# A decoder layer with expert retrieval: the top-16 searches spread over more slots, eight score tiles ahead of the first row group, and 16 KB of the residual stream lent to two more row buffers

## The reference, cut to what matters

```python
h2 = rmsnorm(x2) * (1 + sc2) + sh2
q  = h2 @ w_q                                  # 8 heads x two halves of 128
s1, s2 = scores of each half against 128 keys
v1, i1 = top_k(s1, 16); v2, i2 = top_k(s2, 16)
best, pos = top_k(all 256 sums v1 + v2, 16)    # 16 experts of 16384 for a token and head
gates = softmax(best)
act = gelu(einsum(u_tab[experts], h2))         # one row of 2048 of table u per expert
y   = sum(gates * act * v_tab[experts])        # one row of 2048 of table v per expert
out = rmsnorm(x2 + g2 * y)
```

## Time and profile before

| | |
|---|---|
| median of three runs | 1752.9 us |
| profiled execution | 1751.18 us, span 1749.4 us |
| mean granted clock of TensorE | 0.909 |
| busy: TensorE, VectorE, ScalarE, GpSimd | 1478.3, 1206.5, 542.8, 690.7 us |
| moved by DMA | 624.46 MB, mean 357 GB/s |
| queue of the gathers and of GpSimd's other loads (q0) | 427.52 MB |
| queue of SyncE's loads (q1) | 195.67 MB |

### The profile page before, as it was taken

The page is one execution under the profiler, slowest core; times in us unless marked ns, Lnnn a source line. Parts: engine busy times, 40 slices in busy tenths (PEclk is TensorE's granted clock), DMA queues, the critical chain, the costliest instruction groups (busy, mean ns, idle before and its releaser), DMA issues.

```text
span 1749.4 us, 20157 instructions
## 1 busy us (share of the span) xinstructions
PE 1478.3 (85%) x7320; PEld 980.5 (56%) x7320; DVE 1206.5 (69%) x2134; ACT 542.8 (31%) x1589; POOL 690.7 (39%) x626
## 2 busy tenths in 40 slices
PE   2979999989999998898999757656689899988874
PEld 2558987878788875666676434324333343333331
DVE  5877886879889988898454467768654555445463
ACT  3003442764311247343210146537421010101132
POOL 1000011000122354556676466555654454445461
PEclk9889999999999999999999876667789999998987
DMA  9999997849969679999999899998989999999996
GB/s 337 386 385 407 402 354 308 303 167 370 380 233 359 225 293 379 377 368 397 390 402 396 325 388 379 378 350 319 394 338 406 366 402 400 362 417 389 416 381 249
DMA packets 149806, 624.46 MB, mean 357 GB/s; under 512 B 33994, under 2 KB 38272, under 8 KB 86528
## 3 DMA queue, kind: packets, MB, share of 16 engines
q0 software_dynamic: 82976, 427.52, 62.6%
q1 hardware_dynamic: 66732, 195.67, 29.1%
HBM read 797.54 MB, written 2.10 MB: 457 GB/s over the span
## 4 chain that ended last, share of the span: by engine, by line
PE 31%; DMA 30%; DVE 24%; issue 6%; POOL 5%; ACT 3%; DVEq 1%; SPq 1%; POOLq 0%; ACTq 0%
DMA u_rows<-in_peer_u,expert 23%; DVE u_rows L2033 12%; PE ps L1167 6%; PE ps L1069 5%; PE ps L457 4%; PE ps L912 4%; DVE first_acc L486 3%; DMA v_rows<-in_peer_v,expert_rows 3%; POOL v_rows L801 3%; PE ps L906 2%; PE ps L1219 2%; PE ps L1134 2%; DMA ada_first<-in_w_ada 2%; PE ps L1204 2%; DMA u_rows<-in_peer_v,expert_rows 1%
## 5 line engine op out<-in xcount | busy, mean ns | idle before, releaser
L2033 DVE SCALAR_TENSOR_TENSOR u_rows<-u_rows,h 128x1024 f32<-128x1024 f32 (+1 forms) x416 | 595.3, 1469 | 377.9 <-DMA u_rows<-in_peer_u,expert 374.3
L801 POOL DMA_INDIRECT u_rows<-in_peer_u,expert x256 | 320.6, 1253 | 364.5 <-DVE u_rows L2033 289.5
L801 POOL DMA_INDIRECT v_rows<-in_peer_v,expert_rows x199 | 264.1, 1327 | 162.3 <-PE ps L1167 108.5
L1167 PE MATMUL ps<-v_rows,diag 128*32 128x512 f32 x1592 | 259.4, 693 | 65.1 <-DMA v_rows<-in_peer_v,expert_rows 35.6
L1219 PE MATMUL ps<-dense_rows,dense_weight 128*128 128x512 f32 x640 | 290.6, 612 | 14.9 <-DVE dense_sums L2112 8.2
L457 PE MATMUL ps<-h2T,dense_rows 128*128 128x256 f32 x1280 | 284.0, 383 | 4.2 <-ACT dense_weight L1565 4.1
L457 PEld LDWEIGHTS ps<-h2T,dense_rows 128*128 128x128 f32 x1280 | 243.4, 191 | 52.6 <-issue 17.9
L1219 PEld LDWEIGHTS ps<-dense_rows,dense_weight 128*128 128x128 f32 x640 | 123.1, 196 | 181.9 <-issue 174.9
L1167 PEld LDWEIGHTS ps<-v_rows,diag 128*32 128x32 f32 x1592 | 64.9, 125 | 182.5 <-issue 182.0
L308 POOL DMA_DIRECT2D ada_late<-in_w_ada x61 | 32.4, 531 | 303.7 <-DVE ada_acc L322 260.8
L1204 PE MATMUL ps<-high_hot,low_hot 128*128 128x40 f32 x512 | 82.1, 332 | 78.7 <-issue 54.0
(11 more groups left out here) (308 smaller groups left out, 1874.1 us busy)
## 6 DMA issues: line engine op xcount, KB each, us to landing
ada_late<-in_w_ada POOLq DMA_DIRECT2D x61, 1024.0 KB, 7.8
dense_rows<-in_dense_u SPq DMA_DIRECT2D x40, 1024.0 KB, 8.9
dense_rows<-in_dense_v SPq DMA_DIRECT2D x40, 1024.0 KB, 9.0
ada_first<-in_w_ada SPq DMA_DIRECT2D x64, 512.0 KB, 11.6
ring<-in_w_in SPq DMA_DIRECT2D x10, 2048.0 KB, 23.8
ring<-in_w_o SPq DMA_DIRECT2D x8, 2048.0 KB, 16.8
ring<-in_w_peer_q SPq DMA_DIRECT2D x8, 2048.0 KB, 13.8
opened<-in_w_in SPq DMA_DIRECT2D x8, 1024.0 KB, 13.0
```

The costliest lines, as they stand in the source:

```text
L801: nc.gpsimd.indirect_dma_start(buf[:, :], None, table, bass.IndirectOffsetOnAxis(ap=places, axis=0), bounds_check=last_sparse, oob_is_err= ...
L1167: ins = nc.tensor.matmul(ps[rows, k, :], diag[n % len(diag)][:, :], v_slot(n)[0][:, 512 * k:512 * k + 512], start=first, stop=last)
L2033: ins = nc.vector.scalar_tensor_tensor(out=u_rows[b][:, lo:hi], in0=u_rows[b][:, lo:hi], scalar=1.0, in1=h2[:, q // H, lo:hi], op0=ALU.mul ...
```

## The change

1. `retrieval_slots`: job 1 stands in slots 0 to 11, job 2 in 12 to 26, and jobs 3 to 15 in 5 or 6 slots each from 27 to 95. `exponent(q)` of jobs 2 to 5 moves from the query loop to the slot where its job ends.
2. `tile_key`: the first eight score tiles stand at 30 to 37 instead of 22 to 36; tile 8 and later stay at 22 + 2i.
3. `group_order`: the first row group at 39 instead of 31, 15 groups before slot 107 instead of 19, and 22 instead of 18 from 107 to 168. `gather_key`, `AHEAD` and `SPARE` follow (spare places from v slot 60 instead of 76).
4. x2 is written to a buffer in HBM (2 MB) by SyncE between the last query weights and dense tile 0, and read back before dense piece 40; its 16 KB are two more u buffers for slots 10 to 135. The first use of one waits for the write to land.
5. `spread_weights(q)` waits for diagonals that ScalarE has issued earlier.

```diff
+    park_rows = [at(f"park_rows{b}", A + (96 + 8 * b) * KB, [P, D]) for b in range(2)]
+    parked = nc.dram_tensor("parked", [P, TT, D], F32, kind="Internal").ap()
...
-    LEAD, LAG = 31, 20
+    LEAD, LAG = 39, 20
...
-    LEAD_GROUPS, LAG_GROUPS = (HOT_KEY - LEAD) // QUADS, (HOT_END - LAG) // QUADS
+    LEAD_GROUPS, LAG_GROUPS = 15, (HOT_END - LAG) // QUADS
...
-    SPARE = [(76, 124), (76, 124), (76, 116), (76, TAIL), (REOPENED, TAIL)]
+    PARK = 10, 136
+    SPARE = [(60, 120), (60, 120), (60, 108), (60, TAIL), (REOPENED, TAIL)]
-    AHEAD = 5, 9, 6
+    AHEAD = 3, 7, 6
     def group_order(g):
-        between = HOT_KEY + (g - LEAD_GROUPS) * (HOT_END - HOT_KEY) // (LAG_GROUPS - LEAD_GROUPS)
-        return max(QUADS * g + LAG, min(QUADS * g + LEAD, between))
+        if g < LEAD_GROUPS:
+            return LEAD + g * (HOT_KEY - LEAD) // LEAD_GROUPS
+        return max(QUADS * g + LAG, HOT_KEY + (g - LEAD_GROUPS) * (HOT_END - HOT_KEY) // (LAG_GROUPS - LEAD_GROUPS))
     def gather_key(n):
         if n < 2:
-            return 24
+            return 27
         if n < len(v_rows):
-            return 31
+            return 32
...
-        return max(key, group_order(row_before[n] // QUADS) + 4) if row_before[n] is not None else key
+        return max(key, group_order(row_before[n] // QUADS) + (6 if key < PARK[1] else 4) if row_before[n] is not None else tile_key(DENSE - 1) + 3)
     def tile_key(i):
-        return 22 + 2 * i
+        return 30 + i if i < 8 else 22 + 2 * i
     def retrieval_slots(q):
-        return (5 * q - 5, 5) if q < H else (5 * H - 5 + 4 * (q - H), 4)
+        first = (0, 0, 12, *(27 + 16 * k // 3 for k in range(QJOBS - 2)))
+        return first[q], first[q + 1] - first[q]
...
+    for n in range(SLOTS):
+        open_now = range(len(u_places) if PARK[0] <= n < PARK[1] else len(u_rows))
+        b = min(open_now, key=lambda b: u_slots[b][-1] if u_slots[b] else -1)
...
+            sp.wait_ge(x2_squared, 8)
+            sp.dma_start(parked, x2[:, :, :]).then_inc(x2_loaded, 16)
             sp.wait_ge(ada_steps, 6 * KC - EARLY)
             for s in range(2 * DENSE):
...
+                if s == DENSE:
+                    sp.wait_ge(x2_loaded, 32)
+                    sp.wait_ge(dots, max(u_slots[len(u_rows)][-1], u_slots[len(u_rows) + 1][-1]) + 1)
+                    sp.dma_start(x2[:, :, :], parked).then_inc(x2_loaded, 16)
...
-                if n >= len(u_rows):
-                    pool.wait_ge(dots, n - len(u_rows) + 1)
+                if u_before[n] is not None:
+                    pool.wait_ge(dots, u_before[n] + 1)
+                elif b >= len(u_rows):
+                    pool.wait_ge(x2_loaded, 32)
...
-                if u == 6:
-                    for q in range(2, 5):
-                        exponent(q)
-                if u == 7:
-                    exponent(5)
...
+                if q >= 2:
+                    act.wait_ge(diagonal, TOPK * (q - 1))
...
-                    if n == sum(retrieval_slots(q)) and q >= 6:
+                    if n == sum(retrieval_slots(q)) and q > 1:
                         exponent(q)
...
+                elif c == 0:
+                    dve.wait_ge(x2_loaded, 48)
```

More of the change, by code:

```diff
@@ L553, in build @@
     tail_landed = nc_sem("tail_rows_landed")
+    park_landed = [nc_sem(f"park_rows{b}_landed") for b in range(len(park_rows))]
     groups_used = nc_sem("v_row_groups_used")
@@ L629, in build @@
         row_slots[b].append(n)
+    u_places = list(zip(u_rows + park_rows, u_landed + park_landed))
+    u_slots = [[] for _ in u_places]
+    u_home, u_before = [], []
+    for n in range(SLOTS):
+        open_now = range(len(u_places) if PARK[0] <= n < PARK[1] else len(u_rows))
+        b = min(open_now, key=lambda b: u_slots[b][-1] if u_slots[b] else -1)
+        u_home.append((b, len(u_slots[b])))
+        u_before.append(u_slots[b][-1] if u_slots[b] else None)
+        u_slots[b].append(n)
     def last_before_tail(b):
@@ L637, in v_slot @@
             b = n - LAST
-            return u_rows[b], u_landed[b], 16 * (SLOTS // len(u_rows) + 1)
+            return u_rows[b], u_landed[b], 16 * (len(u_slots[b]) + 1)
         if TAIL <= n < TAIL + 4:
@@ L804, in gather_u @@
             def gather_u(n):
-                b = n % len(u_rows)
+                b, use = u_home[n]
+                buf, landed = u_places[b]
                 if n % TOPK == 0:
@@ L811, in gather_u @@
                     pool.wait_ge(ada_columns, 4)
-                if n >= len(u_rows):
-                    pool.wait_ge(dots, n - len(u_rows) + 1)
-                gather(expert[:, n // TOPK, n % TOPK:n % TOPK + 1], u_rows[b], u_landed[b], peer_u[0])
+                if u_before[n] is not None:
+                    pool.wait_ge(dots, u_before[n] + 1)
+                elif b >= len(u_rows):
+                    pool.wait_ge(x2_loaded, 32)
+                gather(expert[:, n // TOPK, n % TOPK:n % TOPK + 1], buf, landed, peer_u[0])
             def gather_v(n):
@@ L825, in gather_v @@
                 if n >= LAST:
-                    pool.wait_ge(dots, n + 1)
+                    pool.wait_ge(dots, u_slots[n - LAST][-1] + 1)
                 elif TAIL <= n < TAIL + 6:
@@ L2020, in dot @@
             def dot(n):
-                b, use = n % len(u_rows), n // len(u_rows)
+                b, use = u_home[n]
+                rows, landed = u_places[b]
                 q, k = divmod(n, TOPK)
-                dve.wait_ge(u_landed[b], 16 * (use + 1))
+                dve.wait_ge(landed, 16 * (use + 1))
                 if n == 0:
@@ L2032, in dot @@
                 for lo, hi, total in parts:
-                    ins = nc.vector.scalar_tensor_tensor(out=u_rows[b][:, lo:hi], in0=u_rows[b][:, lo:hi], scalar=1.0,
+                    ins = nc.vector.scalar_tensor_tensor(out=rows[:, lo:hi], in0=rows[:, lo:hi], scalar=1.0,
                                                          in1=h2[:, q // H, lo:hi], op0=ALU.mult,
```

## The result

The changed kernel took 1766.2 us (median of 14 runs, 1757.92 to 1773.71), the kernel before 1753.47 us in the same comparison: ratio 1.0069, 95% interval 1.0052 to 1.0085. It is 0.7% slower, where a gain to 1743 was forecast. The profiled execution has a span of 1764.1 us, so its time is close to the median.

What follows compares the result with a forecast made beforehand. DMA was taken as nearest its limit, VectorE as the limit in the first stretch. The profiled 1751.2 - 23 + 14 gave 1742, and the runs' median, 1.7 above that execution, made it 1743 us; range 1716 to 1770.

Steps and rivals of the forecast that it cites:

- Parked stream and thin retrieval: Dots 0 to 32: fewer early retrieval jobs, slot 10's gather waiting for the write; gain 17 us at slot 32, bounds 7 and 25.
- Eight tiles ahead: Start of score tiles: tile 3 waits for ScalarE, group 0 near 681 instead of 642.8, DMA idle some 7 us.
- To tile 39, gain at slot 107: Group 0 to dot 107: three engines mesh, tile 39 ends at 971, dot 107 at 996; gain 23 us, bounds 8 and 40.
- Slots 107 to 168: Moved v gathers and x2's read-back come here: 2 us until slot 136, 12 behind it; loss 14 us, bounds 0 and 32.
- "2 us" for dots 107 to 135: Four moved v gathers, 2.8 MB, cost 7.5 us less what six u buffers fill, so 2 us.
- Behind dot 168: 0: From dot 168 to the end: order unchanged, 466 us as before, so no gain or loss.
- Retrieval behind slot 32 at nothing: Later retrieval jobs, to slot 96: hidden by DMA, counted at 0; without that cover 10.1 us a job.
- Rival B: Behind slot 107: seven v buffers set 12.9 us a group, 165 to 170 us from 137 to 168; 1768 us, chance 0.24.
- Rival A: Whole phase: idle DMA time fills, gain 38 us to slot 107, loss 5 behind it; 1720 us, chance 0.22.
- Rival C: Whole phase: it only trades, added bytes and new idle time use up the first stretch's gain; 1753 us, chance 0.16.

Runs made afterwards that it cites:

- after_early: The changed kernel with the write of x2 issued ahead of the last two query weights instead of behind them; 1751.6 us, ratio 0.9991 to the kernel before.
- thin_order: The changed kernel without parking: four u buffers, no write or read of x2, v gathers issued two slots earlier; 1753.1 us, ratio 0.9993 to the kernel before.
- thin_back: The kernel before with thin retrieval and 15 row groups before slot 107, score tiles and first group placed as before; 1740.4 us, ratio 0.9926.
- thin_only: The kernel before with the thin retrieval alone; group order, tiles and buffers as before; 1735.2 us, ratio 0.9900.
- thin_half: The kernel before with thin retrieval, each score tile contracting over half of the channels, all transfers kept; 1734.8 us, ratio 0.9902.

## Why the prediction was wrong, by its own steps

- *Parked stream and thin retrieval.* The gather for slot 10 was put at 555, dot 10 at 563.5 and dot 32 at 636; measured 555.3, 564.6 and 637.3. Right, and the write landed 15.7 us after its issue at 539.3. The stall was in the sum; what it costs was put at 8 us there (a gain of 17 instead of 25 at slot 32). Without it (after_early) dot 32 comes 18.7 us sooner after dot 0, and the end 13.7 us sooner.
- *Eight tiles ahead.* Group 0 at 681 with TensorE waiting for ScalarE before tile 3: measured 683.3 and a wait of 8.5 us. Right as a time. Its price was put at 7 us of idle DMA; from dot 0, thin_order reaches dot 107 6.9 us behind thin_back, which differs from it by these tiles and group 0.
- *To tile 39, gain at slot 107.* Forecast 971 and 996 (gain 23 us), measured 980.3 and 1004.7 (14.8, of which 1.5 is an earlier dot 0, within the spread of the table's profiles). This failed by 8 us. I took three engines near their limit to mesh in 286 us from group 0 to tile 39; it took 293.4, and DMA ran at 356 GB/s from dot 32 to dot 107, not at the 381 that was the lower of my two rates. The 25 us from tile 39 to dot 107 were right (24.4). Moving 16 gathers out between dots 32 and 107 was to give 6 us beyond dot 32; it gave none.
- *Slots 107 to 168: "I take the middle, 12 us"; loss 14.* Measured 25.0 (288.6 against 263.6), of which 22.9 behind dot 135. This is the step that failed most, and it is a term of the wrong size in two ways. The bytes: 9 gathers and the read-back, 8.4 MB, were to fall behind slot 136. By issues it was 13 gathers of v and 3 of u more, by rate and time 11.4 MB, and the read-back was not among them, as it had landed before dot 135. The idle time: at 392 GB/s the forecast lets 9 of the 21 us go into it, and it took in 6 of 29. The "2 us" for dots 107 to 135 came out (2.1), with the read-back in it that had been put elsewhere, so by luck.
- *Behind dot 168: 0.* Measured 4.5 us in the profile (470.8 against 466.3), and 0.6 in after_early. Not explained; the profiles of all kernels lie between 461.8 and 470.8 there.
- *Retrieval behind slot 32 at nothing.* In thin_only dots 32 to 107 took 372.9 us against 366.6, so 6 of the 23 us gained before dot 32 were given back. It is one execution of each, and the runs do not say to what.

Together 8 + 11 + 5 us: 1742 becomes 1766.

**Rival B** named the place and the price (166.7 us from dot 135 to 168, "165 to 170"; 1768), with 0.24, and the sign that was to speak for it, more than 160 us there, came. Its mechanism, seven v buffers turning over in 12.9 us a group, is not what the trace shows. There GpSimd would wait for row groups; in that stretch it waited 17.3 us for them to free a v buffer, against 15.8 before, while TensorE's waits for rows of v to land grew from 12.1 to 43.5 us and a gather into `v_rows` took 11.9 us to land (median) instead of 8.7. That points to late transfers and not to missing buffers, but no run varied the number of v buffers, so B's mechanism is made unlikely and not ruled out. **Rival A** has nothing for it. **Rival C**, that moves only trade idle time, gives the time of thin_order (0.9993), not that of the change.

The rule of the Trainium skill cited against the place of the write ("DMA: Bandwidth & Descriptors", section "Rules for kernel authors": issue early, wait late) agrees with the trace and after_early: the write was issued at 539.3, GpSimd had come to its wait at 533.2, and issuing it earlier was worth 13.7 us. What the same page of the Trainium skill says of the order within a ring (section "Queues, rings and completion order") agrees too: the query weights issued at 538.9 landed 11.2 us later, near 550.1, the write behind them near 555.0 and the first dense tile behind it near 557.1.

What stays open is how the cost of the order divides between the eight tiles ahead and the moved groups: 7 us of it is seen at dot 107, in single profiles, and the two alone are too cheap for the intervals to say more.

## What to carry to other kernels

A transfer that is moved is priced at both ends: what its bytes cost where it goes, and what they free where it leaves, up to the point where the next engine becomes the limit. Here 16 gathers (29 us of bytes) gave back 7 to 14 us by dot 107 and cost 18 behind it. To price the first end, count the bytes from the order of issue, with every transfer in the stretch that it is really issued in. A DMA share of 0.91 is not 9% of room: of 13 us idle, 6 could be filled. And a combined change is best measured part by part: the thin retrieval alone was 1% faster and hidden inside a change that was 0.7% slower.

## What the runs showed of the hardware

- Score tiles with half of the matmuls (TensorE busy 106.5 of 176.2 us instead of 171.9 of 184.4 from dot 32 to 67) changed the total of a kernel whose DMA share was 0.95 to 0.99 between dots 32 and 100 by nothing that could be measured (thin_half 0.9902 against thin_only 0.9900, each uncertain by 0.3%).
- The write of 2 MB to HBM, issued 0.4 us behind a load of 2 MB, landed after 15.7 us; three loads of 1 MB behind it took 18.4 us (median). These rows are of 530 to 560 us in the kernel after:

```profile
dense_rows<-in_dense_u SPq DMA_DIRECT2D x3, 1024.0 KB, 18.4
parked<-x SPq DMA_DIRECT2D x1, 2048.0 KB, 15.7
```
